# The head norm of the retention branch worked inside the stage of the input projections

## The reference

```python
h = layer_norm(ALPHA * x + 0.5 * swiglu(x, ...))
proj = h @ w_in
rq, rk, rv, rg, fq, fk, fv, fl, mq, gl = jnp.split(proj, SPLIT_IDX, axis=-1)
ro, ret_state = retention(rotary(rq), rotary(rk) * (DK_R ** -0.5), rv, ret_s0)
ret_out = (jax.nn.silu(rg) * head_norm(ro, ret_gn_g)) @ w_ret_o
logf = jax.nn.log_sigmoid(fl + b_forget)          # forget gates of the second branch

def head_norm(o, g):                              # o: tokens x 4 heads x 128
    mu = jnp.mean(o, axis=-1, keepdims=True)
    var = jnp.mean(jnp.square(o - mu), axis=-1, keepdims=True)
    return (o - mu) * lax.rsqrt(var + GN_EPS) * g
```

## Time and profile before

| | us |
|---|---|
| median of 3 runs | 3667.02 |
| the runs | 3665.63, 3673.86, 3667.02 |
| the profiled execution, its own time | 3673.46 |
| its span, first to last instruction | 3671.6 |
| mean granted TensorE clock | 0.949 of full speed |

### The profile page before, as it was taken

One profiled execution on the slowest core, in us unless ns is written; L12 is line 12 of the kernel. 1 busy time (PEld: TensorE's weight loads), 2 busy tenths in 40 slices (PEclk: granted clock), 3 DMA queues, 4 the chain that ended last, 5 costly groups with the idle time before them and its releaser, 6 DMA issues. The chain is left out here.

```text
span 3671.6 us, 56105 instructions
## 1 busy us (share of the span) xinstructions
PE 3314.7 (90%) x21121; PEld 2999.5 (82%) x21121; DVE 888.4 (24%) x1581; ACT 625.5 (17%) x1163; POOL 794.6 (22%) x696
## 2 busy tenths in 40 slices
PE   5999999997988898786799899999796999999996
PEld 5999999996887798554688666666686999999995
DVE  2111111114206211555101022222314111111114
ACT  3000000002101100344000144434203000000003
POOL 0232222323120131022111111111021223233220
PEclk8999999998997899899899999999798999999998
DMA  5111111111110112210211299999311111111111
GB/s 141 35 51 40 42 49 34 49 49 29 29 44 22 41 40 67 91 48 17 52 43 43 60 297 307 300 305 303 121 29 29 34 46 50 33 51 43 37 37 55
DMA packets 328667, 293.12 MB, mean 80 GB/s; under 512 B 33640, under 2 KB 249064, under 8 KB 328048
## 3 DMA queue, kind: packets, MB, share of 16 engines
q1 hardware_dynamic: 317136, 275.93, 24.3%
q0 software_dynamic: 11424, 15.76, 1.6%
HBM read 279.34 MB, written 12.26 MB: 79 GB/s over the span
## 5 line engine op out<-in xcount | busy, mean ns | idle before, releaser
L207 PE MATMUL f_acc<-x_hi,w_hi_last 128*128 128x364 f32 x1056 | 233.5, 329 | 27.5 <-SPq L489 27.5
L165 POOL CAST w_hi_first<-w_raw_first 128x1024 fp32r<-128x1024 f32 (+1 forms) x96 | 82.9, 863 | 738.4 <-issue 301.3
L207 PE MATMUL f_acc<-x_hi,w_hi_first 128*128 128x364 f32 x1056 | 233.5, 329 | 6.9 <-SPq L489 6.9
L207 PE MATMUL f_acc<-x_lo,w_hi_last 128*128 128x364 f32 x1056 | 234.0, 330 | 0.0
L207 PE MATMUL f_acc<-x_hi,w_lo_last 128*128 128x364 f32 x1056 | 234.0, 330 | 0.0
L207 PE MATMUL f_acc<-x_hi,w_lo_first 128*128 128x364 f32 x1056 | 233.9, 330 | 0.0
L207 PE MATMUL f_acc<-x_lo,w_hi_first 128*128 128x364 f32 x1056 | 233.7, 329 | 0.0
L207 PEld LDWEIGHTS f_acc<-x_hi,w_hi_last 128*128 128x128 f32 x1056 | 184.0, 189 | 28.0 <-issue 28.0
L165 POOL CAST w_hi_last<-w_raw_last 128x1024 fp32r<-128x1024 f32 (+2 forms) x92 | 73.5, 799 | 614.2 <-PE f_acc L207 610.2
L596 DVE SCALAR_TENSOR_TENSOR br<-f_acc,br 128x1092 f32 x88 | 114.1, 1296 | 368.8 <-PE f_acc L207 368.8
L207 PEld LDWEIGHTS f_acc<-x_hi,w_hi_first 128*128 128x128 f32 x1056 | 184.0, 189 | 7.1 <-issue 7.1
(11 more groups left out here) (399 smaller groups left out, 6321.8 us busy)
## 6 DMA issues: line engine op xcount, KB each, us to landing
br<-cache_fox_k SPq DMA_DIRECT2D x256, 256.0 KB, 5.6
br<-cache_fox_v SPq DMA_DIRECT2D x256, 256.0 KB, 6.5
w_raw_first<-w_ffn_gate SPq DMA_DIRECT2D x22, 512.0 KB, 3.8
w_raw_first<-w_ffn_up SPq DMA_DIRECT2D x22, 512.0 KB, 3.8
w_raw_last<-w_ffn_gate SPq DMA_DIRECT2D x22, 512.0 KB, 3.8
w_raw_last<-w_ffn_up SPq DMA_DIRECT2D x22, 512.0 KB, 3.8
w_raw_first<-w_ffn_down SPq DMA_DIRECT2D x40, 256.0 KB, 2.9
w_raw_last<-w_ffn_down SPq DMA_DIRECT2D x40, 256.0 KB, 2.8
```

Source lines behind the costliest of these rows:

```text
L165: self.nc.gpsimd.tensor_copy(hi, raw).then_inc(self.high[s], 1)
L207: mm = self.nc.tensor.matmul(out[:, b, 0:width], w[s][:, k, :], x[:, k, b * width:(b + 1) * width], start=(k == 0 and first), stop=(k == k ...
```

## The change

The stage `phase_head_norm` is gone. Its work is cut into 12 units (4 heads x 3 token blocks), and unit u is worked on between tiles u and u+1 of `phase_attention_in`: its mean behind the products of tile u, its variance behind those of tile u+1. The variance matmul now has the full matrix of 1/128 as weights and 364 columns, so it gives the variance to all channels at once; root and reciprocal are taken on 364 columns, and the diagonals and the spreading matmuls are no longer there. The tiles come in another order, since fq overwrites the rows of the retention's output: fl, then fk and fv (tiles 1 to 8), mq (9 to 12), fq (13 to 16), whose readers also wait for the units of their row. The loops over tiles are written out for all engines. `ga`, the raw forget gates, now lies in a row of `g.fkv`, and the transposes of the forget gates use the variance's PSUM bank.

```diff
-def phase_head_norm(g):
...
-            @block.tensor
-            def _(pe):
-                def means(h):
-                    if h > 0:
-                        pe.wait_ge(centred, h)
-                    for b in range(NB):
-                        mm = nc.tensor.matmul(mean[:, b, 0:TB], mean_w[:], g.br[:, 8 + h, b * TB:(b + 1) * TB],
-                                              start=True, stop=True)
-                    mm.then_inc(mean_ok, 1)
-
-                def variances(h):
-                    pe.wait_ge(squared, h + 1)
-                    if h > 0:
-                        pe.wait_ge(std_ok, h)
-                    for c in range(TC):
-                        mm = nc.tensor.matmul(var[:, h % 2, c:c + 1], sq[h % 2][:, starts[c]:starts[c] + P],
-                                              mean_w[:, 0:1], start=True, stop=True)
-                    mm.then_inc(var_ok, 1)
-
-                def spreads(h):
-                    pe.wait_ge(diag_ok, h + 1)
-                    if h > 0:
-                        pe.wait_ge(used, h)
-                    for c in range(TC):
-                        mm = nc.tensor.matmul(rstd[:, c * P:(c + 1) * P], g.ones[:], diag[h % 2][:, c, :],
-                                              start=True, stop=True)
-                    mm.then_inc(spread, 1)
...
 def phase_attention_in(g, neg_d):
-
     nc, io, w = g.nc, g.io, g.w
-    fox, mq = 6, 2
-    pairs = fox + mq
+    KV, MQ, FQ = 1, 9, 13
+    TILES = 17
+    UNITS = H_R * NB
...
+        ga = g.fkv[0:H_F, 6, :]
...
+        mean_w, eps = g.sb(ctx, "hn_mean_w", [P, P]), g.sb(ctx, "hn_eps", [P, 1])
+        sq, std = ([g.sb(ctx, f"hn_{x}{s}", [P, TB]) for s in range(2)] for x in ("sq", "std"))
         acc = [g.ps(ctx, f"a_acc{s}", [P, NB, 512]) for s in range(2)]
-        lfn_ps = g.ps(ctx, "lfn_ps", [P, NCH + 1, H_F])
+        mean, var = g.ps(ctx, "hn_mean", [P, 512]), g.ps(ctx, "hn_var", [P, 512])
+        lfn_ps = var[:, 0:(NCH + 1) * H_F].rearrange("p (c h) -> p c h", h=H_F)
...
+        def columns(i):
+            if i == 0:
+                return C_FL
+            if i < MQ:
+                return C_FQ + (4 + i - KV) * P
+            return C_MQ + (i - MQ) * P if i < FQ else C_FQ + (i - FQ) * P
+
+        def target(i):
+            if i < MQ:
+                return g.fkv[:, i - KV, :], 1.0
+            return (g.br[:, 4 + i - MQ, :], 1.0) if i < FQ else (g.br[:, 8 + i - FQ, :], DF ** -0.5)
+
+        def unit(u):
+            h, x = divmod(u, NB)
+            cols = slice(x * TB, (x + 1) * TB)
+            return g.br[:, 8 + h, cols], g.br[:, h, cols], g.gn_g[:, h:h + 1]
...
+                for i in range(TILES):
+                    at = columns(i)
+                    w.load(sp, i % 2, i // 2 + b[i % 2], io["w_in"][:, at:at + P], KD)
...
+                nc.gpsimd.memset(mean_w[:], 1.0 / P).then_inc(ready, 1)
+                nc.gpsimd.memset(eps[:], EPS).then_inc(ready, 1)
+                for i in range(2, TILES):
+                    w.split(pool, i % 2, i // 2 + b[i % 2], KD)
...
-                with pe.Fori(0, pairs) as n:
-                    for s in range(2):
-                        pe.wait_ge(free[s], n + 1)
-                        w.products(pe, s, n + (b0, b1)[s], KD, acc[s], g.xh, g.xl)
-                pe.wait_ge(free[0], pairs + 1)
-                w.products(pe, 0, pairs + b0, KD, acc[0], g.xh, g.xl)
+                def head_mean(u):
+                    if u > 0:
+                        pe.wait_ge(centred, u)
+                    nc.tensor.matmul(mean[:, 0:TB], mean_w[:], unit(u)[0], start=True, stop=True).then_inc(mean_ok, 1)
+
+                def head_variance(u):
+                    pe.wait_ge(squared, u + 1)
+                    if u > 0:
+                        pe.wait_ge(std_ok, u)
+                    nc.tensor.matmul(var[:, 0:TB], mean_w[:], sq[u % 2][:], start=True, stop=True).then_inc(var_ok, 1)
+
+                for i in range(TILES):
+                    pe.wait_ge(free[i % 2], i // 2 + 1)
+                    w.products(pe, i % 2, i // 2 + b[i % 2], KD, acc[i % 2], g.xh, g.xl)
+                    if i == 0:
+                        pe.wait_ge(ready, 2)
+                    if i < UNITS:
+                        head_mean(i)
+                    if 0 < i <= UNITS:
+                        head_variance(i - 1)
                 pe.wait_ge(scanned, 1)
+                pe.wait_ge(std_ok, UNITS)
...
+                def square(u):
+                    act.wait_ge(centred, u + 1)
+                    if u >= 2:
+                        act.wait_ge(var_ok, u - 1)
+                    nc.scalar.activation(sq[u % 2][:], unit(u)[0], ACT.Square).then_inc(squared, 1)
+
+                def deviation(u):
+                    act.wait_ge(var_ok, u + 1)
+                    if u >= 2:
+                        act.wait_ge(normed, u - 1)
+                    nc.scalar.activation(std[u % 2][:], var[:, 0:TB], ACT.Sqrt, bias=eps[:]).then_inc(std_ok, 1)
+
+                for i in range(TILES):
+                    if i % 2 == 0 and i > 0:
+                        dst, scale = target(i)
+                        act.wait_ge(w.done[0], i // 2 + b[0] + 2)
+                        if i >= FQ:
+                            act.wait_ge(normed, NB * (i - FQ + 1))
+                        nc.scalar.mul(blocks_of(dst), acc[0][:, :, 0:TB], scale).then_inc(free[0], 1)
+                    if i < UNITS:
+                        square(i)
+                    if 0 < i <= UNITS:
+                        deviation(i - 1)
...
+                def centre(u):
+                    x = unit(u)[0]
+                    dve.wait_ge(mean_ok, u + 1)
+                    nc.vector.tensor_tensor(x, x, mean[:, 0:TB], ALU.subtract).then_inc(centred, 1)
+
+                def finish(u):
+                    x, y, gain = unit(u)
+                    r = std[u % 2]
+                    dve.wait_ge(std_ok, u + 1)
+                    nc.vector.reciprocal(r[:], r[:])
+                    n_chain.mark(nc.vector.scalar_tensor_tensor(y, x, gain, y, ALU.mult, ALU.mult))
+                    n_chain.wait(dve)
+                    nc.vector.tensor_tensor(y, y, r[:], ALU.mult).then_inc(normed, 1)
+
+                def forget_sums():
+                    dve.wait_ge(a_steps, 3)
+                    chain.mark(nc.vector.scalar_tensor_tensor(lf[:], ga, 0.0, gb[:], ALU.min, ALU.subtract))
+                    chain.wait(dve)
+                    chain.mark(nc.vector.memset(ga, 1.0))
+                    chain.wait(dve)
+                    nc.vector.tensor_tensor_scan(gb[:, 0:TP], ga[:, 0:TP], lf[:, 0:TP], 0.0, ALU.mult, ALU.subtract)\
+                        .then_inc(scanned, 1)
+
+                for i in range(TILES):
+                    if i == 0:
+                        dve.wait_ge(w.done[0], b[0] + 2)
+                        nc.vector.tensor_scalar(blocks_of(ga), acc[0][0:H_F, :, 0:TB], g.b_forget[:], None, ALU.add)\
+                            .then_inc(free[0], 1)
+                    elif i % 2:
+                        dst, scale = target(i)
+                        dve.wait_ge(w.done[1], i // 2 + b[1] + 2)
+                        if i >= FQ:
+                            dve.wait_ge(normed, NB * (i - FQ + 1))
+                        nc.vector.tensor_scalar(blocks_of(dst), acc[1][:, :, 0:TB], scale, None, ALU.mult).then_inc(free[1], 1)
+                    if i < UNITS:
+                        centre(i)
+                    if 0 < i <= UNITS:
+                        finish(i - 1)
+                    if i == 3:
+                        forget_sums()
...
             phase_retention(g)
-            g.end_phase()
-            phase_head_norm(g)
             g.end_phase()
```

More of the change, by code:

```diff
@@ L1439, in _ @@
             def _(pool):
-                with pool.Fori(1, pairs) as n:
-                    for s in range(2):
-                        w.split(pool, s, n + (b0, b1)[s], KD)
-                w.split(pool, 0, pairs + b0, KD)
+                nc.gpsimd.memset(mean_w[:], 1.0 / P).then_inc(ready, 1)
+                nc.gpsimd.memset(eps[:], EPS).then_inc(ready, 1)
+                for i in range(2, TILES):
+                    w.split(pool, i % 2, i // 2 + b[i % 2], KD)
             @block.tensor
             def _(pe):
-                with pe.Fori(0, pairs) as n:
-                    for s in range(2):
-                        pe.wait_ge(free[s], n + 1)
-                        w.products(pe, s, n + (b0, b1)[s], KD, acc[s], g.xh, g.xl)
-                pe.wait_ge(free[0], pairs + 1)
-                w.products(pe, 0, pairs + b0, KD, acc[0], g.xh, g.xl)
+                def head_mean(u):
[16 more added lines that the diff above has]
+                        head_variance(i - 1)
                 pe.wait_ge(scanned, 1)
+                pe.wait_ge(std_ok, UNITS)
                 for c in range(NCH + 1):
@@ L1464, in _ @@
                 chain = Chain(a_steps)
-                chain.mark(nc.scalar.activation(gb[:], ga[:], ACT.Abs))
```

(38 more changed lines are left out.)

97 lines of the change are left out of this document (3 added, 94 removed).

## The result

The changed kernel takes 3654.56 us (median of 7 runs, 3650.10 to 3659.86). The kernel before took 3673.86 us in 7 runs beside them (3665.63 to 3678.75); the ratio is 0.995, 95% interval 0.9935 to 0.9964. It is faster, by 19.3 us where 23.2 had been summed up, and the time lies 0.56 us above the range of the prediction.

A forecast was written before the change was run, and what follows sets the result against it. PE (TensorE) alone was taken to set the projections' time, while the head norm stage was worth its whole length. -38.4 + 14.7 + 0.5 = -23.2 us gave a forecast of 3645 us, range 3637 to 3654.

The forecast's parts named there:

- The removed stage: Head norm stage with its barrier goes, so the projections' first weight load starts 38.4 us earlier.
- The units on PE: In the projections, 24 plain f32 matmuls at 0.612 us each add 14.7 us of PE time.
- The bound from below (8.0): The 24 unit matmuls would cost 8.0 us if they ran like fp32r products, in two passes.
- the 0.2 us at each wait (19.5): Upper estimate for the units: each of 24 matmuls loses another 0.2 us at its wait, 19.5 us in all.
- The cover: Unit matmuls are waited for 12 us after becoming possible, some 9 us of cover, so DVE and ACT work costs nothing.
- POOL's splits: Weight splits in the projections, even stretched by 1.1 us to 4.6 of a 13.2 us tile, cost nothing.
- the 1 us for tile 3: At the extreme, POOL standing still for all DVE time, tile 3 takes 14.5 us and gives back about 1 us once.
- Straight code: Rival: PE stalls fetching the projections' written-out tiles, 9 us at worst (3654); slower only from 2.8 us a packet; 3%.
- End of the stage: Eight more semaphores cleared between the two barriers at the projections' end add 0.5 us.
- The base: Starting time of the whole kernel: profiled 3673.46 gives 3650.3, median 3667.02 gives 3643.8; 3645 us was taken.
- serial units: Rival: projection matmuls wait for their own unit's DVE and ACT work, 12 x 2 = 24 us, no change, 3668; 4%.
- Part given back: Rival: late splits, a longer slow start, some 0.2 us at each wait cost 5 to 10 us, 3650 to 3655; 13%.

The follow-up runs named there:

- the kernels with none, one and two sets: Changed kernel without units or any head norm (ratio 0.9901), unaltered (0.995), and with each unit's mean and variance matmul issued twice (0.9992).
- the early weights: Changed kernel, plus the projections' first two weight tiles loaded and split during the retention, its buffers moved to make room: 3645.66 us, ratio 0.9927.
- the two pairs: Changed kernel with first weights loaded during retention, split early or later, each without and with rounded fp32r variance: 3645.66 and 3645.42 us; 3643.12 and 3638.76 us.

## Why the prediction was off, by its own steps

**The removed stage** held: 38.42 us in the first pair of traces and 37.4 in the second for 38.4, and 38.2 and 38.0 us of in-stage gain in the two profiles of the kernel without head norm.

**The units on PE** held: 14.25 us in the first pair of traces, 14.7 to 15.1 in the kernels with none, one and two sets, for 14.7. The bound from below (8.0) and the 0.2 us at each wait (19.5) are both excluded.

**The cover** held, and it was a real condition: without it the stage takes 28.3 us more, and the gain is gone.

**POOL's splits** were not touched: 2.40 us, not 3.52. The sentence of the Trainium skill (GPSIMD Engine Reference, Key points) that DVE's instructions with two SBUF inputs contend with POOL was right in kind, but here the splits and such instructions never ran at the same time, so the changed kernel did not put it to the test, nor the 1 us for tile 3; and in the early weights it was DVE that stood still. The Trainium skill's page SBUF — State Buffer (Who interferes with whom) says more: the shared ports are an exclusive lock, and the order of issue decides who blocks. The trace agrees: DVE's first delayed instruction ends 0.27 us behind POOL's first cast (1130.76 and 1130.49), and the pair of L1235 as long behind the second (1134.41 and 1134.14). So does the kernel before: there DVE's two-operand L1496 began 0.04 us ahead of POOL's subtraction, and it was the subtraction that took 3.52 us.

**Straight code** cost nothing that can be told (1.0001, 0.9991 to 1.0011), as taken.

**End of the stage** held: 0.52 us for 0.5.

**The base is the step that failed**: "the median of the three runs shown is 3667.02, 6.4 less, and gives 3643.8", and the lean to 3645 from it. Over 71 runs the kernel before takes 3673.2 us on average with a spread of 4.0 (one standard deviation) for a single run; the three shown had two from its lower edge. With 3673.2 as the base the same sum gives 3650.0, inside the range. Part of this was the draw: the mean of all four times shown, 3670.0, was still 3 us low. The profiled execution's 3673.46, the other base in the text, less 23.2 gives 3650.3, inside the range and 4.3 us below the result.

**The size of the sum** was off by the rest. Each term is right where it was placed, yet the time moved 20.1 us, 3.1 less than the 23.2 they add up to, and the sum put what the stages behind do at nothing. The gap is somewhat larger than its error (0.8 us for the time; the stage's gain rests on profiles 2.5 us apart). Where it arises and why stays open: it goes neither with the units nor with one stretch behind the stage.

**The rivals.** Straight code and serial units did not happen, and each had a kernel of its own: the first showed none of the up to 9 us that the rival allowed for, the second 28.3 us in the stage for its 24. Part given back, 3650 to 3655 us, is what the time reads, but by luck: none of its three mechanisms acted.

## What to carry to other kernels

A short serial stage can go into the gaps of a long stage that one engine bounds, at the price of what it adds to that engine alone, provided each step of a unit stands a whole tile behind the step it waits for; the same units without that distance made this kernel slower than before. When the first transfer and split of the next stage are moved into the stage ahead, look at which engine is on the path there: here GpSimd's cast and subtraction held up VectorE's two-operand instructions until they were done, so such work belongs where VectorE waits anyway. And a prediction should start from the mean of as many executions as there are, the profiled one among them, when they scatter by 8 us and the range is 17 wide.

## What the runs showed of the hardware that was not expected

- VectorE's instructions with both operands in SBUF took 1.10 to 2.56 us instead of 0.42 beside GpSimd's cast and subtraction, which themselves lost at most 0.19 us; 5.6 us of work were lost in a stretch of 7.7. A TENSOR_SCALAR with one tensor in SBUF and a column of factors (L1273) was held up too, 2.42 instead of 0.34 us. In the changed kernel the subtraction of the means (one operand in PSUM) kept its 0.51 to 0.54 us and the reciprocal its 2.43 beside the same splits.
- A plain f32 matmul of 364 columns cost 0.61 to 0.63 us of TensorE's time, the rounded one 0.12 to 0.17 (12 of them saved 5.9 and 5.3 us in the two pairs), so under a third.
- Two profiled executions of one kernel differed by 11 us in the stages behind an unchanged seam (2207.2 and 2218.1 us), 7 of them in d_ktp's stage (481.8 and 488.7).
- The granted clock over the same 75 us of the same 328 matmuls was 0.89 and 0.91 in two profiles of the kernel before and 0.89 and 0.86 in two of the kernel without head norm: a step of 0.02 to 0.03 between two kernels with a profile each says nothing.
